# A mixture of experts on one core: 32 tokens of its first layer take their U rows by gather, TensorE runs four steps ahead of a search's end, and the loads between the U and V phases change places

## What is computed

```python
def peer(h, w_pq, sub_keys, u_tab, v_tab):        # h: tokens x 1024
    q = (h @ w_pq).reshape(B, T, 8, 2, 64)
    s = einsum('bthcd,hckd->bthck', q, sub_keys)   # 128 keys in each half
    top_s, top_i = top_k(s, 16)
    cand = top_s[..., 0, :, None] + top_s[..., 1, None, :]
    best_s, best_j = top_k(cand.reshape(..., 256), 16)
    expert = i1 * 128 + i2                         # 8 heads x 16 experts per token
    w = softmax(best_s)
    u = u_tab[expert]; act = gelu(einsum('cd,ced->ce', h, u))
    return einsum('ce,ced->cd', act * w, v_tab[expert])
```

## Time and profile before

| | |
|---|---|
| median of 3 runs | 3246.27 us (3245.52 to 3247.68) |
| the profiled execution | 3238.48 us, with a span of 3236.4 us |
| PE busy | 3009.5 us, 93% |
| DVE busy | 2451.3 us, 76% |
| ACT busy | 1536.5 us, 47% |
| POOL busy | 942.6 us, 29% |
| layer 0: U phase; V phase | 394.4 to about 1068 us; about 1068 to 1592 us |
| layer 1: U phase; V phase | about 1852 to 2266 us; about 2266 to 2560 us |
| mean granted clock of PE | 0.958 |

### The profile page before, as it was taken

One profiled execution on the slowest core, in us unless ns is written; L12 is line 12 of the kernel. 1 busy time (PEld: TensorE's weight loads), 2 busy tenths in 40 slices (PEclk: granted clock), 3 DMA queues, 4 the chain that ended last, 5 costly groups with the idle time before them and its releaser, 6 DMA issues.

```text
span 3236.4 us, 49042 instructions
## 1 busy us (share of the span) xinstructions
PE 3009.5 (93%) x19164; PEld 2657.7 (82%) x19164; DVE 2451.3 (76%) x4976; ACT 1536.5 (47%) x2895; POOL 942.6 (29%) x835
## 2 busy tenths in 40 slices
PE   6998999999999999999979899899999999988898
PEld 4656799989999888888765899888998899755898
DVE  2696588897888688888758678897999866668654
ACT  3455335737557333333444547496555543232543
POOL 0000046565656344344000024454685200000000
PEclk9999999999999999999998999999999999967899
DMA  7384347969789999999527568899999867501444
GB/s 233 97 283 157 127 159 273 341 242 315 271 286 339 370 371 353 381 357 368 174 96 256 182 227 315 278 351 361 380 400 400 325 207 247 158 33 47 155 142 132
DMA packets 352934, 824.41 MB, mean 255 GB/s; under 512 B 20256, under 2 KB 216384, under 8 KB 332608
## 3 DMA queue, kind: packets, MB, share of 16 engines
q1 hardware_dynamic: 257216, 469.79, 41.8%
q0 software_dynamic: 93120, 347.17, 29.3%
q10 hardware_dynamic: 2368, 4.32, 0.4%
HBM read 747.76 MB, written 73.40 MB: 254 GB/s over the span
## 4 chain that ended last, share of the span: by engine, by line
PE 65%; DVE 22%; DMA 6%; ACT 4%; issue 2%; POOL 1%; DVEq 0%; SPq 0%; ACTq 0%; POOLq 0%
PE ps L1021 16%; PE ps L944 16%; PE ps L639 13%; DVE fr L1823 5%; DVE area L1831 4%; DVE area L1823 3%; DMA ring<-in_peer_v 3%; PE ps L1000 3%; PE ps L1109 2%; PE ps L717 2%; PE ps L1101 2%; PE ps L873 2%; DVE plain L2259 1%; ACT fr L1265 1%; PE ps L919 1%
## 5 line engine op out<-in xcount | busy, mean ns | idle before, releaser
L1823 DVE TENSOR_TENSOR fr<-ring,fr 128x1024 fp32r<-128x1024 f32 x641 | 781.7, 1222 | 473.3 <-ACT fr L1265 470.5
L1265 ACT CAST fr<-ring 128x1024 fp32r<-128x1024 f32 x677 | 703.7, 1045 | 566.5 <-PE ps L1021 323.5
L944 PE MATMUL ps<-fr 128*128 128x384 f32 (+1 forms) x4784 | 851.0, 331 | 14.2 <-DVE fr L1823 14.1
L944 PEld LDWEIGHTS ps<-fr 128*128 128x128 f32 x4784 | 789.2, 191 | 19.5 <-DVE fr L1823 17.1
L1021 PE MATMUL ps<-fr 128*128 128x512 f32 x2304 | 523.9, 390 | 4.4 <-DVE fr L1823 4.4
L1021 PEld LDWEIGHTS ps<-fr 128*128 128x128 f32 x2304 | 433.4, 188 | 94.8 <-ACT area L1582 4.7
L639 PE MATMUL ps<-fr 128*128 128x256 f32 (+1 forms) x2928 | 415.3, 304 | 26.2 <-DVE fr L1823 26.2
L639 PEld LDWEIGHTS ps<-fr 128*128 128x128 f32 x2928 | 389.1, 193 | 52.3 <-DVE fr L1823 32.5
L2680 POOL DMA_INDIRECT plain<-in_peer_v,area x192 | 284.9, 1484 | 259.6 <-DVE area L1831 167.0
L1046 PE MATMUL ps<-fr 128*128 128x384 f32 x1024 | 297.6, 362 | 12.9 <-DVE fr L1823 12.4
L2712 POOL DMA_DIRECT2D g_scratch<-area x224 | 127.0, 567 | 581.1 <-ACT area L1582 540.9
(11 more groups left out here) (228 smaller groups left out, 3990.5 us busy)
## 6 DMA issues: line engine op xcount, KB each, us to landing
ring<-in_peer_uT SPq DMA_DIRECT2D x128, 1024.0 KB, 6.2
ring<-in_peer_v SPq DMA_DIRECT2D x128, 1024.0 KB, 10.0
ring<-in_w_mod SPq DMA_DIRECT2D x48, 1024.0 KB, 5.3
w_scratch<-acc POOLq DMA_DIRECT2D x36, 1024.0 KB, 8.4
g_scratch<-area POOLq DMA_DIRECT2D x128, 192.0 KB, 5.2
area<-g_scratch POOLq DMA_DIRECT2D x64, 384.0 KB, 8.8
area<-w_scratch POOLq DMA_DIRECT2D x16, 1536.0 KB, 10.0
ring<-in_w_ada SPq DMA_DIRECT2D x24, 1024.0 KB, 5.1
```

Of the source, the lines that this page charges most:

```text
L944: ins = e.matmul(o[:, 0:width], pairs[m][0], pairs[m][1], start=(m == 0), stop=(l == 0 and m == last), skip_group_check=l == 1)
L1265: e.copy(hi, x).then_inc(act.after(("high", name)), 1)
L1823: return e.tensor_tensor(o, a, b, op).then_inc(dve.after(*labels), 1)
```

## The change

- `EXTRA = (32, 0)`: tokens 128 to 159 of layer 0 take their U results from gathers: 32 more gathers and as many row sums, `N_ROWS = (160, 64)`. Their V part stays dense. The products of layer 0's U phase now have 352 columns.
- The gathered rows go main 0 to 15, extra 0 to 31, main 16 to 127. The extra ones use `idx2`, made of block 1's indices, and `hx2`, a copy of the extra tokens' inputs laid out four times over; their sums go through a small transpose (`xt`) and GELU, and are multiplied into their weights. In the stored GELU results they have ones.
- The extra tokens' quads move from the start to the end: block 1 has 24 quads, block 2 has 32, block 3 has 40, of which the last 8 are extra and built by DVE alone (four L1828 operations for two, none by ACT).
- `AHEAD_STEPS`: PE makes 4 steps between the 28 and the wait for `ww`, and 4 fewer after the next search's first product, in both layers; ACT makes 3 in layer 1.
- Memory: `cand` shares the space of `eq`, four `SW` buffers shrink; `GL[2]` and `GL[3]` now overlap `hx`, so their first loads wait for the last U row.
- The loads between the phases come in another order, and V rows 1 to 7 are no longer issued at once.
- The turns are spread anew: in the 28 steps of t = 1, 2, 3 lie 7, 9, 11 rows (6, 9, 7 before), in the 14 steps and quads 33, 42, 50 (33, 33, 33 before), in the last 22 steps 8 (7 before).

The core of the diff:

```diff
+AHEAD_STEPS = {"pe": (4, 4), "act": (0, 3)}
+EXTRA = (32, 0)
+FIRST_EXTRA = 16
+N_ROWS = tuple(n + x for n, x in zip(GATHERED, EXTRA))
+def quads_of(l, t):
+    n = max(0, 128 * (t + 1) - max(GATHERED[l], 128 * t)) // 4
+    x = EXTRA[l] // 4
+    return n - x if t == 1 and n else n + x if t == 3 else n
...
-                pairs = M.three(lambda s, k: v[s][:, k, :], lambda s, k: HR[:, s, k, b.first:T], range(8))
+                pairs = M.three(lambda s, k: v[s][:, k, :], lambda s, k: HR[:, s, k, b.first + EXTRA[l]:T], range(8))
...
-                fill(fill_a)
+                fill(fill_a - (early_steps if h4 == 0 else 0))
             fill(2 * fill_b)
             fill(2 * fill_c)
             if 128 * (t + 1) <= b.first:
                 continue
+            early_steps = AHEAD_STEPS["pe"][l]
+            fill(early_steps)
+            if (l, t) == (0, 2):
+                n = EXTRA[l]
+                w.wait_ge(dve, ("urow", l, FIRST_EXTRA + n - 1))
...
             w.wait_ge(dve, ("ww", l, t))
...
+        for i in range(2 if EXTRA[l] else 0):
+            w.wait_ge(pe, ("hx2", l, i))
+            e.copy(b.hx2[:, 512 * i:512 * i + 512], ps(("hx2", l, i))[:, :]).then_inc(act.after(("hx2", l, i)), 1)
...
+            if (l, t) == (0, 1):
+                w.wait_ge(dve, ("more experts", l))
+                n = EXTRA[l]
+                for r in range(1, 128 // n):
+                    e.dma_start(b.idx2[n * r:n * r + n, 0:n], b.idx2[0:n, n * r:n * r + n]).then_inc(
+                        M.moved.after(("more experts",)), 16)
...
-        fill(5)
+        fill(5 + 5 * l)
         w.wait_ge(pe, ("ow", l, D // 4 - 1))
         w.wait_ge(dve, ("oh", l, D // 4 - 1))
         load_g(KEPT[l] // 2 + 0)
-        fill(5)
         for i in range(2):
             w.wait_ge(M.w_stored[i], ("w", l, nst - 2 + i))
         load_w(0)
+        fill(5)
+        load_g(KEPT[l] // 2 + 1)
+        fill(5)
+        load_w(1)
         fill(3)
-        load_g(KEPT[l] // 2 + 1)
-        load_w(1)
-        fill(5)
-        load_g(KEPT[l] // 2 + 2)
-        load_g(KEPT[l] // 2 + 3)
+        if l == 1:
+            load_g(KEPT[l] // 2 + 2)
+            load_g(KEPT[l] // 2 + 3)
...
         w.wait_ge(pe, ("pu", l, 127))
-        for k in range(len(b.v_rows)):
-            v_row(k)
+        if l == 0:
+            w.wait_ge(dve, ("urow", l, N_ROWS[l] - 1))
+            load_g(2)
+            load_g(3)
+        v_row(0)
         for a in range(128):
+            if a + 1 < len(b.v_rows):
+                v_row(a + 1)
```

More of the change, by code:

```diff
@@ L87, in _u_turns @@
     for t in range(2 if l == 1 else 4):
-        begin, quads = step + search, (128 * (t + 1) - GATHERED[l]) // 4 if t == 0 else 32
+        begin, quads = step + search, quads_of(l, t)
         step = begin + (rest + quads * fill_w if quads else 2 * fill_c)
@@ L417, in peer @@
         b.iT = lay.take(4 * D).rearrange("p (c t) -> p c t", c=4)
-        b.SW = [lay.take(256) for _ in range(4)]
+        b.SW = [lay.take(128) for _ in range(4)]
         b.TS = lay.take(256).rearrange("p (h r) -> p h r", r=16)
@@ L437, in peer @@
         if l == 0:
+            b.hx2 = lay.take(1024)
+            b.idx2 = lay.take(128).bitcast(U32)
+            b.dot2, b.gel2 = lay.take(EXTRA[0]), lay.take(EXTRA[0])
             self.u_rows[0] += [b.qT[:, t].rearrange("p k q -> p (k q)") for t in range(2)]
@@ L907, in peer @@
             transposes(o, [M.ACC[:, 4 * i + k, 0:128] for k in range(4)]).then_inc(pe.after(("hx", l, i)), 1)
+        for i in range(2 if EXTRA[l] else 0):
+            w.wait_ge(dve, ("h2", l, 4 * i + 3))
+            o = bank(("hx2", l, i), (act, ("hx2", l, i)))
+            transposes(o, [M.ACC[:, 4 * i + k, 128:256] for k in range(4)]).then_inc(pe.after(("hx2", l, i)), 1)
         def u_plain(a, steps):
@@ L943, in u_product @@
                     width = D if l == 0 or m % 2 == 1 else 2 * D
-                    ins = e.matmul(o[:, 0:width], pairs[m][0], pairs[m][1], start=(m == 0), stop=(l == 0 and m == last),
+                    ins = e.matmul(o[:, EXTRA[l]:width], pairs[m][0], pairs[m][1], start=(m == 0), stop=(l == 0 and m == last),
                                    skip_group_check=l == 1)
@@ L989, in peer @@
                 continue
+            early_steps = AHEAD_STEPS["pe"][l]
[3 more added lines that the diff above has]
+                w.wait_ge(dve, ("urow", l, FIRST_EXTRA + n - 1))
+                o = bank(("xt", l), (act, ("xt", l)))
+                for q in range(4):
+                    ins = e.matmul(o[n * q:n * q + n, 0:n], b.dot2, M.c("ident")[:, n * q:n * q + n], start=True,
+                                   stop=True)
+                ins.then_inc(pe.after(("xt", l)), 1)
             w.wait_ge(dve, ("ww", l, t))
@@ L1614, in peer @@
                 continue
+            early_steps = AHEAD_STEPS["act"][l]
+            fill(early_steps)
+            if (l, t) == (0, 2):
+                w.wait_ge(pe, ("xt", l))
+                e.activation(b.gel2, ps(("xt", l))[:, 0:EXTRA[l]], ACT.Gelu).then_inc(act.after(("xt", l)), 1)
             w.wait_ge(pe, ("ti", l, t))
@@ L2210, in choose @@
             tt(ww, ww, of_sum, M_, ("ww", l, t))
+        if (l, t) == (0, 1):
+            stt(b.R1f, b.I1, 128.0, b.I2, M_, AD)
+            last()
+            e.tensor_copy(b.idx2, b.R1f).then_inc(dve.after(("more experts", l)), 1)
+        if (l, t) == (0, 2):
+            w.wait_ge(act, ("xt", l))
+            tt(b.iT[:, 2, 0:EXTRA[l]], b.iT[:, 2, 0:EXTRA[l]], b.gel2, M_, ("xw", l))
     def one_hot(l, quad):
         b = M.peers[l]
-        half, tok = quad % 2, 4 * quad
+        half, tok = quad % 2, 4 * QUADS[l][quad]
         w.wait_ge(act, ("it", l, M.block_of(l, quad)))
+        extra = tok < EXTRA[l]
+        if extra:
+            w.wait_ge(dve, ("xw", l))
         if quad >= 2:
@@ L2246, in peer @@
             ts(M.ACC[:, k, 0:n], M.ACC[:, k, 0:n], M.MOD[l][:, 24 + k, 0:1], None, AD, None, ("h", ("peer", l), k))
+        n = EXTRA[l]
+        for k in range(8 if n else 0):
+            ts(M.ACC[:, k, 128 + n:256].rearrange("p (r t) -> p r t", t=n),
+               M.ACC[:, k, 128:128 + n].unsqueeze(1).to_broadcast([128, 128 // n - 1, n]), M.MOD[l][:, 24 + k, 0:1], None,
+               AD, None)
+            last()
+            ts(M.ACC[:, k, 128:128 + n], M.ACC[:, k, 128:128 + n], M.MOD[l][:, 24 + k, 0:1], None, AD, None, ("h2", l, k))
+        if n:
+            for x in b.GS:
+                e.memset(x[:, 0:n], 1.0).then_inc(dve.after(), 1)
+            dve.note(("ones", l))
         def u_low(a):
@@ L2290, in peer @@
             fill(fill_c)
-            for quad in range(t0 // 4, (128 * (t + 1) - b.first) // 4):
+            for _ in range(quads_of(l, t)):
                 one_hot(l, quad)
+                quad += 1
                 fill(fill_w)
@@ L2745, in peer @@
                     u_row(k)
-            t0 = max(0, 128 * t - b.first)
-            for n in range(t0 // 16, (128 * (t + 1) - b.first) // 16):
+            for n in range(group, group + quads_of(l, t) // 4):
                 fill(4 * fill_w)
```

76 lines of the change are left out of this document (53 added, 23 removed).

## The result

The change makes the kernel slower: a median of 3254.35 us over 11 runs (3245.21 to 3261.56), against 3244.02 us for the kernel before (11 runs, 3234.88 to 3247.68) on the same chip. The ratio is 1.0043, with a 95% interval of 1.0033 to 1.0053. The forecast was 3237 us with "faster" the likeliest, so its sign is wrong, though 3254 lies in its range. The profiled execution has a span of 3246.8 us, 10.4 us more than 3236.4.

What follows compares the result with a forecast made beforehand. PE was taken to bound the quads and DVE the searches; +1 - 3 - 6 + 2 + 1 - 4 = -9 us took the span from 3236.4 to 3227 and the median from 3246.3 to 3237, range 3214 to 3258.

Steps and rivals of the forecast that it cites:

- I take the ring's 360: Layer 0's three stretches of fillings and quads: 360 us for 366.4, a term of -6, between -18 and +9.
- PE's pace: Fillings and quads at the matmuls' own speed: 348.6 us; as a rival 3216 us in all, chance 0.18.
- DVE's busy time: Fillings and quads: 300.7 us of work plus 30 for 26 row sums and 5, 336, with 30 left for waits.
- ring of four: Four row buffers beside the quads: lag 3.3 plus landing 8.2 us, over four, 2.88 a row, 360 for 125 rows.
- DMA, if it were a wall: Fillings and quads: 133.2 MB at 355 GB/s take 375 us; at 401 GB/s it would be 332.
- the rival: Ring of four rows too short: landing 10 us, loop 12.5, quads 391 us, whole 3268, slower; chance 0.15.
- the searches: Layer 0's searches t = 2 and t = 3: 0 and +2 us, between 0 and +4 together.
- DMA full: Rival: transfers at their limit beside the quads, 375 us there, +9 for -6, whole 3252; chance 0.13.
- The start: Before layer 0's U products: +1 us, for ACT's two copies of `hx2` ahead of the first `u_high`.
- the first 144 steps: Layer 0's U phase before the fillings and quads: -3 us, between 0 and -8; PE gets 9.3 faster.
- The seam: Between layer 0's U and V phases: +1 us, between -2 and +5; last two gathers stand behind `load_w(0)`.
- Layer 1: -4 us, between 0 and -8: -3 at PE's second wait for `ww`, -1 from the loads between the phases.

Runs made afterwards that it cites:

- deepthin: The changed kernel with both two more row buffers in layer 0 and row sums over 128 of 1024 columns: 3201.02 us in two executions, ratio 0.9865.
- after: The kernel with the whole change, against the kernel before it: 3254.35 us, ratio 1.0043.
- thin: The changed kernel with layer 0's row sums over 128 of 1024 columns, gathers whole: 3221.17 us, ratio 0.9939.
- deep: The changed kernel with two more row buffers in layer 0, five from the second stretch of quads, six from the third: 3224.57 us, ratio 0.9954.
- ahead0: The changed kernel with AHEAD_STEPS at zero on PE and ACT, in both layers: 3262.97 us, ratio 1.0064.

## Why the prediction was wrong

**The step that failed** is "I take the ring's 360", out of "Four bounds", for a term of -6 us that measured +16.7. Each bound was about right when it stood alone, the ring's only in its sum:

| bound | forecast | measured | where |
|---|---|---|---|
| PE's pace | 348.6 | 349.7, or a little less | `deepthin` |
| DVE's busy time | 336 | 334.7 | after, 84.96 + 111.58 + 138.13 |
| ring of four | 360 | 364.4, with a short sum; lag and landing of after alone give 334 | `thin`, after |
| DMA, if it were a wall | 375 | none at that height | 366 to 404 GB/s in `deep`, `deepthin` |

But the largest of them was taken for the answer, as if they were independent. They aren't: the row sum that waits for a gather stands in DVE's stream ahead of remainders and one-hots, so a wait for a row is added to DVE's work; and while DVE does that work, a row that has landed lies in its buffer, 1.8 us on average, so the next gather starts later. The prediction's loop, 3.3 and 8.2 us, had no term for this. DVE's 334.7 us and its 42.6 us of waits for rows make 377.3 of the 386.5 us. The prediction had "30 left for its waits" and saw what stood behind L2259, but used it only in the rival. Taking away either half, the ring's (`deep`, -23.6) or DVE's (`thin`, -22.1, which shortens the lag too), cures most of it, and both together lead to PE's pace.

**The landing time** is not the second half of it. The 8.2 us of the earlier trace rows are one of two lines of that view; the other, for the buffers `plain`, has 13 gathers at 8.6, and over the three stretches the mean before is 7.8. With 26 more gathers in them it became 8.6, while the lag fell from 3.1 to 2.1, as the prediction said it would once DVE waits. The rival had 10 us, a loop of 12.5, 3.13 us a row and 391 us; the trace shows a loop of 12.3, 3.09 and 386.5. So this rival, with a chance of 0.15, told what happened: DVE waits at its row sums, and one-hots and PE behind it. But its number is in part luck, since the missing time came from rows that lie ready, and not from a landing of 10. It gave 3268 because it took +25 there, where +16.7 came, and it had no gain in the searches.

**DMA full**: wrong as a mechanism. The share was 0.95 to 0.98 in after at 340 to 356 GB/s, and still `deep` moved the same bytes at 366 to 388. What the Trainium skill says, page "DMA: Bandwidth & Descriptors", section "Where 436 GB/s comes from", that about 358 GB/s per core binds, is not borne out here: this core held 401 GB/s over 110 us and 404 over 80. The Trainium skill's page "HBM Reference", section "Specifications (TRN2)", puts 358 GB/s down as the share of a core whose neighbour streams too, and about 425 GB/s for a core that streams alone; with this reading, which the prediction left out, the trace agrees. A share near 1 meant that the queues held work all the time, not that no more could go through.

**Point by point.** The start (+1.2) and the first 144 steps (-3.8) came as forecast. The matmul of 352 columns was cheaper by 14 to 15 ns for 13.4 in the quads, and by 7 in the long run of the first search. In the searches the steps ahead counted for too little: for t = 2 nothing, for t = 3 one wait for a key product. `ahead0` shows what that misses, since with them away the searches come to -1.6 and +1.7 us, close to the forecast's 0 and +2, and the steps ahead take another 3.3 and 2.7 us off. (That DVE is the busier engine in both searches is also misread: in the second has PE 68.13 and DVE 62.66 us.) PE's wait for `ww` doesn't only cost while it lasts: as the prediction's own first paragraph says, products behind it run slowly, 13.68 us for 66 of 384 columns, with a granted clock of 0.50 from 725.4 to 728.0 us, where after, with a wait of 0.58 us and a clock of 1.00 behind it, has these:

```profile
692.99 11.11 PE L981 MATMUL ps<-fr 128*128 128x352 f32 x66
```

They also put PE behind in the next search, where DVE waits for its key products. The seam came at +2 for +1. In after's trace the gathers behind `load_w(0)` end it, as feared, but `deep` has the same order and a tail of 25.5 us, so the late rows of a short ring are as likely the reason.

**Layer 1** was forecast at -4 and gave +0.9. The wait itself shrank as expected, from 7.02 us to this:

```profile
2105.48 0.90 PE L677 MATMUL ps<-con,area 128*128 128x128 f32 x3 [2.67 <-DVE area L1883]
```

The second search got 1.8 us shorter (94.3 to 92.5), and the quads behind it 1.7 us longer (112.7 to 114.4); in `ahead0` the two stand at 94.3 and 112.6. So steps taken ahead there are given back in the quads. What holds PE in those quads is not DVE but ACT's copies. Waits of PE, 2105 to 2222 us after, and 2096 to 2212 us before:

```profile
PE ps L992 <- ACT area_r L1617: 7.5, 14, 0.8
PE ps L1048 <- DVE area L1888: 0.6, 1, 0.6
```

```profile
PE ps L1000 <- DVE area L1828: 2.6, 6, 0.4
PE ps L955 <- ACT area_r L1566: 2.4, 7, 0.3
```

In `ahead0` the waits for ACT are 2.1 us again. Whether PE's four steps or ACT's three bring them, no run here tells.

## What to carry to other kernels

- Bounds of engines that hand work to each other in order may add. Where an engine waits, in order, for something that it has itself to release, reckon its busy time plus the waits, and give the loop of a buffer a term for the time that a landed row lies behind other work; the largest single bound is right only while the waiter has slack. Read the slack first: 62 us of waits for ACT hid the rows before, 3 us did after.
- Before load is added to a ring of buffers, work out at which loop it turns, and assume that landing grows with the load (7.8 us before, 8.6 after). A landing time read from a few gathers that were waited for is too long: 10.2 us against a mean of 8.6. Then look for memory that is free for part of the time: here two buffers out of finished queries turned 0.4% slower into 0.5% faster.
- A DMA share near 1 is no proof of a wall. More transfers under way at once is the test.
